# A two-block transformer kernel: another order of work in the opening of its first weight product

## What is computed

```python
def first_block(x, c, ada_w, ada_b, pre_g, post_g, sgu_w_in, ...):
    cond = jax.nn.silu(c)
    for i in range(DEPTH):
        mod = cond @ ada_w[i] + ada_b[i]
        shift, scale, gate = jnp.split(mod, 3, axis=-1)
        h = rms_norm(x, pre_g[i]) * (1 + scale[:, None, :]) + shift[:, None, :]
        ...
        y = sgu_mixer(h, sgu_w_in[j], ...)

def sgu_mixer(h, w_in, norm_g, w_s, b_s, w_out):
    u, v, z = jnp.split(h @ w_in, 3, axis=-1)
    ...
```

## Time and profile before

| | |
|---|---|
| median of 3 runs | 2480.13 us (2478.33 to 2480.51) |
| the profiled execution | 2477.93 us |
| its span | 2476.1 us |
| TensorE busy | 2433.2 us, 98% |
| VectorE busy | 1889.0 us, 76% |
| ScalarE busy | 1399.4 us, 57% |
| GpSimd busy | 442.0 us, 18% |
| granted TensorE clock, mean | 0.999 |

### The profile page before, as it was taken

How to read it: one execution, slowest core, us unless ns; L and a number is a source line. 1 busy time by engine, 2 the same in 40 slices (tenths; PEclk the granted TensorE clock), 3 DMA queues, 4 the chain that set the end, 5 groups by cost and what they waited for, 6 DMA issues and landing times.

```text
span 2476.1 us, 31108 instructions
## 1 busy us (share of the span) xinstructions
PE 2433.2 (98%) x11597; PEld 2018.7 (82%) x11597; DVE 1889.0 (76%) x2295; ACT 1399.4 (57%) x1934; POOL 442.0 (18%) x298
## 2 busy tenths in 40 slices
PE   6999999999999999998999999999999999999999
PEld 5888888888887989887888888888888888888887
DVE  7899798977777787866655555557988878788884
ACT  6655765444447555555566676755655545555553
POOL 0264563111020000110000000043111021111111
PEclk9999999999999999999999999999999999999999
DMA  9999677978784877754555556455465555646454
GB/s 364 321 341 349 237 256 273 336 283 290 271 313 149 246 212 220 233 208 149 167 173 163 177 153 183 157 187 187 155 236 170 204 187 191 217 170 221 170 203 154
DMA packets 370999, 549.47 MB, mean 222 GB/s; under 512 B 31405, under 2 KB 158129, under 8 KB 370225
## 3 DMA queue, kind: packets, MB, share of 16 engines
q1 hardware_dynamic: 368688, 539.54, 64.6%
q10 hardware_dynamic: 1824, 6.04, 0.7%
q0 software_dynamic: 352, 2.11, 0.2%
HBM read 545.53 MB, written 2.11 MB: 221 GB/s over the span
## 4 chain that ended last, share of the span: by engine, by line
PE 88%; DVE 8%; ACT 2%; issue 1%; DMA 1%; SPq 0%; POOL 0%; DVEq 0%; ACTq 0%; POOLq 0%
PE ps L2393 48%; PE ps L2398 24%; DVE lo L1305 3%; PE ps L2423 2%; PE ps L2419 2%; PE ps L2420 2%; DVE ps L1330 1%; PE ps L2379 1%; PE ps L2378 1%; PE ps L2380 1%; DVE lo L1282 1%; DMA raw<-in_sgu_w_in 1%; PE ps L3007 1%; PE ps L2655 1%; ACT hi L630 1%
## 5 line engine op out<-in xcount | busy, mean ns | idle before, releaser
L1305 DVE TENSOR_TENSOR lo<-raw,hi 128x1024 fp32r<-128x1024 f32 x550 | 706.9, 1304 | 350.8 <-ACT hi L630 350.2
L630 ACT ACTIVATE hi<-raw 128x1024 fp32r<-128x1024 f32 x550 | 571.3, 1051 | 431.3 <-PE ps L2398 352.7
L2393 PE MATMUL ps<-hi,a_hi 128*128 128x512 f32 (+1 forms) x2016 | 798.6, 396 | 2.1 <-issue 0.9
L2393 PE MATMUL ps<-hi,a_lo 128*128 128x512 f32 (+1 forms) x2016 | 785.6, 390 | 0.0
L2398 PE MATMUL ps<-lo,a_hi 128*128 128x512 f32 (+1 forms) x2016 | 539.0, 389 | 1.5 <-DVE lo L1305 1.5
L616 ACT ACTIVATE hi<-raw 128x1024 fp32r<-128x1024 f32 x339 | 358.2, 1060 | 292.7 <-PE ps L2398 255.2
L1282 DVE TENSOR_TENSOR lo<-raw,hi 128x1024 fp32r<-128x1024 f32 x339 | 424.4, 1272 | 107.2 <-ACT hi L616 105.0
L2393 PEld LDWEIGHTS ps<-hi,a_hi 128*128 128x128 f32 x2016 | 378.7, 188 | 85.1 <-issue 5.3
L2398 PEld LDWEIGHTS ps<-lo,a_hi 128*128 128x128 f32 x2016 | 378.4, 188 | 81.1 <-DVE lo L1305 1.9
L2393 PEld LDWEIGHTS ps<-hi,a_lo 128*128 128x128 f32 x2016 | 378.9, 188 | 74.4
L2393 PE MATMUL ps<-hi,b_hi 128*128 128x512 f32 x880 | 347.4, 395 | 0.6 <-ACT y L1015 0.3
(11 more groups left out here) (351 smaller groups left out, 2436.6 us busy)
## 6 DMA issues: line engine op xcount, KB each, us to landing
raw<-in_sgu_w_in SPq DMA_DIRECT2D x88, 1024.0 KB
raw<-in_ada_w SPq DMA_DIRECT2D x64, 1024.0 KB
raw<-in_w_up SPq DMA_DIRECT2D x64, 1024.0 KB
raw<-in_w_down SPq DMA_DIRECT2D x64, 1024.0 KB
raw<-in_w_in SPq DMA_DIRECT2D x42, 1024.0 KB
raw<-in_ada_w SPq DMA_DIRECT2D x64, 512.0 KB
raw<-in_sgu_w_out SPq DMA_DIRECT2D x32, 1024.0 KB
raw<-in_w_in SPq DMA_DIRECT2D x128, 256.0 KB
```

The costliest lines, as they stand in the source:

```text
L630: nc.scalar.activation(hi[:, q % CHUNKS, 0:width], raw[:, r % RAWS, q % 2 * CW:q % 2 * CW + width], ACT.Copy).then_inc(hi_ready, 1)
L1305: nc.vector.tensor_tensor(lo[:, q % CHUNKS, 0:width], raw[:, r % RAWS, q % 2 * CW:q % 2 * CW + width], hi[:, q % CHUNKS, 0:width].bitcast( ...
L2393: nc.tensor.matmul(ps[:, 2 * s + t, 0:width], x[:, k0 + j, t * P:(t + 1) * P], hi[:, c, w], start=begins, stop=False)
```

## The change

- **Head.** c goes to `acc_s` instead of `tf`, so SyncE no longer waits for GpSimd before it. The second half of x is issued by SyncE, behind slabs (0, 0) and (0, 1), with a semaphore of its own; the eight small vectors follow behind it. VectorE copies the small vectors only after all four sums of group 0.
- **x in pieces.** ScalarE normalises the first 512 columns of both halves, and the other 1536 later, between the first chunks. TensorE turns two groups of x before the first chunk (before: five) and the other six after chunks 1, 2, 3, 8, 9 and 10 (`XT_AFTER`; before: three, after chunks 1, 2 and 3).
- **Blocks.** LATE is 6: the first six chunks are one turn each, all of group 0. `GROUP_AFTER`, `SUMMED_AFTER` and the loads of the last slabs ("s") have new places. On ScalarE, `modulated(1)` stands in the turn of the loop for chunk 4 as before, but chunk 4 now ends a turn.
- **VectorE.** `modulated(0)` stands ahead of the first two lo; `split(0)` stands behind lo of chunk 0, then slab (1, 0), then lo of chunk 1.
- **Spatial turns** stand after chunks 43, 49, 55 and 61 instead of 45, 49, 53 and 57.

```diff
-GROUPS, LATE = 8, 4
-GROUP_AFTER = {4: 1, 14: 2, 24: 3, 36: 4, 46: 5, 58: 6, 66: 7}
+GROUPS, LATE = 8, 6
+GROUP_AFTER = {5: 1, 14: 2, 24: 3, 34: 4, 44: 5, 54: 6, 62: 7}
...
-    order = [(j, 0) for j in range(LATE)] + [(4, 0), (5, 0), (4, 1), (5, 1)] + [(j, h) for j in range(6, PHASE_W) for h in range(2)]
+    order = [(j, 0) for j in range(LATE)] + [(LATE + e, h) for h in range(2) for e in range(2)]
+    order += [(j, h) for j in range(LATE + 2, PHASE_W) for h in range(2)]
...
-XT_BANKS = (3, 4, 2, 3, 4, 4, 4, 4)
+XT_BANKS = (3, 4, 4, 4, 4, 4, 4, 4)
+XT_AFTER = (1, 2, 3, 8, 9, 10)
...
-            sp.wait_ge(set_up, 2)
-            sp.dma_start(ra[A_C:A_C + 16], d["c"].rearrange("a (r q) -> (a r) q", q=P)).then_inc(first_landed, 16)
+            sp.dma_start(c_rows, d["c"].rearrange("a (r q) -> (a r) q", q=P)).then_inc(first_landed, 16)
...
-                if r == 1:
+                if r == 2:
+                    sp.dma_start(x[:, 1, :], d["x"][0, P:2 * P, :]).then_inc(x1_landed, 16)
+                    sp.wait_ge(set_up, 2)
                     for place, source in small:
...
             x_turned(0)
+            x_turned(1)
             hi_next(act, n, 0)
+            modulated(0)
             hi_next(act, n, 1)
-            x_turned(1)
-            modulated(0)
+            normal(0, NB, D)
             hi_next(act, n, 2)
-            for g in range(2, 5):
-                x_turned(g)
-            group_at = {c + (c > 4): g for c, g in GROUP_AFTER.items()}
+            normal(1, NB, D).then_inc(n_out, 1)
+            group_at = {c + (1 if g > 1 else -1): g for c, g in GROUP_AFTER.items()}
             for q, (m, j, h, begins, ends) in enumerate(OPENING):
                 p = m // PHASE_W
                 act_steps(act, n, 1)
+                if q - 1 in XT_AFTER:
+                    x_turned(2 + XT_AFTER.index(q - 1))
...
             ada_sum(dve, n, 0, acc, early)
+            ada_sum(dve, n, 1, acc, early)
+            first_var()
+            ada_sum(dve, n, 2, acc, early, between=first_rstd)
+            ada_sum(dve, n, 3, acc, early)
             dve.wait_ge(vec_turned, 2)
             nc.vector.tensor_copy(va[:, KT:A_ROWS], ps[:, 4, KT:A_ROWS]).then_inc(vec_kept, 1)
             nc.vector.tensor_copy(vb[:, :], ps[:, 4, P:P + B_ROWS]).then_inc(vec_kept, 1)
-            ada_sum(dve, n, 1, acc, early, between=first_var)
-            ada_sum(dve, n, 2, acc, early, between=first_rstd)
-            ada_sum(dve, n, 3, acc, early)
...
+            modulated(0)
+            opening_lo(0)
+            split(0)
+            n.raw.base += 1
+            ada_sum(dve, n, 0, acc_s, early)
+            n.raw.base -= 1
+            opening_lo(1)
...
-            pe.wait_ge(n_out, 2)
-            x_turned(2)
             pe_ada(pe, n)
-            x_turned(3)
-            x_turned(4)
-            unread(0, 3)
+            unread(0, 5)
...
-                if 1 <= q < 4:
-                    x_turned(4 + q)
+                if q in XT_AFTER:
+                    pe.wait_ge(n_out, 2)
+                    x_turned(2 + XT_AFTER.index(q))
```

More of the change, by code:

```diff
@@ L194 @@
 OPENING = opening_chunks()
-SPATIAL_AFTER = tuple(next(q for q, c in enumerate(OPENING) if c.turn == 2 * PHASE_W + j and c.ends) for j in range(0, 8, 2))
-XT_BANKS = (3, 4, 2, 3, 4, 4, 4, 4)
+SPATIAL_AFTER = tuple(next(q for q, c in enumerate(OPENING) if c.turn == 2 * PHASE_W + j and c.ends) for j in range(0, PHASE_W, 3))
+XT_BANKS = (3, 4, 4, 4, 4, 4, 4, 4)
+XT_AFTER = (1, 2, 3, 8, 9, 10)
 def opening_slabs():
@@ L206, in opening_slabs @@
             slabs.append(sums.pop(0))
-        if FIRST - PHASE_W <= w < FIRST - PHASE_W + LAST_A:
-            slabs.append(("s", w - FIRST + PHASE_W))
+        if w in LAST_SUMMED_AFTER:
+            slabs.append(("s", LAST_SUMMED_AFTER.index(w)))
     assert not sums
@@ L863, in modulated @@
             def modulated(g):
+                act.wait_ge(xt_kept, g + 1)
                 act.wait_ge(scales, g + 1)
@@ L1674, in end_of_block @@
                                                    in1=rstd[:, :], op0=ALU.mult, op1=ALU.mult).then_inc(centred, 1)
-            ready = {c + 3 - (c == 4): g for c, g in GROUP_AFTER.items()}
+            ready = {c + (3 if g > 1 else 1): g for c, g in GROUP_AFTER.items()}
             last_ends = {q: c.block for q, c in enumerate(OPENING) if c.ends and c.turn >= 3 * PHASE_W}
@@ L1690, in opening_lo @@
                     end_of_block(last_ends[q - AHEAD])
-            for slab in OPENING_SLABS[4:]:
-                if slab[0] == "w":
-                    w = slab[1]
-                    opening_lo(2 * w)
-                    opening_lo(2 * w + 1)
-                    if w == 0:
-                        modulated(0)
-                else:
-                    out_ = acc if slab[0] == "s" else (acc, acc_s)[slab[1] % 2]
-                    ada_sum(dve, n, slab[-1], out_, early, between=(lambda: split(0)) if slab == ("a", 1, 0) else None)
+            modulated(0)
[5 more added lines that the diff above has]
+            opening_lo(1)
+            for slab in OPENING_SLABS[6:]:
+                if slab[0] == "w":
+                    opening_lo(2 * slab[1])
+                    opening_lo(2 * slab[1] + 1)
+                else:
+                    ada_sum(dve, n, slab[-1], acc if slab[0] == "s" else (acc, acc_s)[slab[1] % 2], early)
             for q in range(2 * FIRST, 2 * FIRST + AHEAD):
@@ L2596, in x_turned @@
             def x_turned(g):
-                if g >= 3:
-                    pe.wait_ge(xt_kept, g - 2 if g < 5 else g)
+                if g >= 2:
+                    pe.wait_ge(xt_kept, g)
                 for k in range(2 * g, 2 * g + 2):
```

29 lines of the change are left out of this document (15 added, 14 removed).

## The result

| | before | after |
|---|---|---|
| median | 2480.32 us (2478.33 to 2482.56, 6 runs) | 2498.47 us (2496.57 to 2500.05, 6 runs) |
| profiled execution | 2477.93 us | 2500.05 us |
| its span | 2476.1 us | 2498.2 us |

The ratio is 1.0072, with an interval of 1.0059 to 1.0085: slower by 18.2 us. The forecast was 2490.9, with a range up to 2497.

A forecast was written before the change was run, and what follows sets the result against it. TensorE, busy for 98% of the span, was taken to bound the kernel. The terms 0.2 + 5.6 + 0.3 + 3.2 + 1.3 + 0.2 gave 10.8 us more, 2490.9 us on the median, range 2484 to 2497.

The forecast's parts named there:

- Step 1: Head: the first chunk comes no sooner, at about 29.7, since TensorE's turning waits for VectorE's small-vector copies; +0.2 us.
- Step 2: Before chunk 3: the fifth slab's place is freed late, the load queue runs dry; +5.6 us, +0.3 one slab later.
- Step 3: Before chunk 6: TensorE waits for a turn's taking out, behind the second modulation on ScalarE; +3.2 us.
- 4, three more turnings: Between the first chunks: six groups of x are turned there instead of three, 3 x 0.44; +1.3 us.
- Step 5: Rest of the opening: 2.6 us of new wait, against old waits of 1.5 and 0.9 going; net +0.2 us.
- The extra 0.3 one slab later: Part of the supply hole: slab 3 lands at 46.4, its rounding and copy end just after TensorE ends chunk 3; +0.3 us.
- rival B: TensorE's clock slows after each of the two new waits: 4.8 us more, 2495.7; chance 13%.
- its term for VectorE's extra work: Ahead of chunk 44: one slab of ada_w more (24 instead of 23) on VectorE without slack; 2.6 us of wait.
- Rival C: VectorE falls behind in the dense stretch, by the upper bound for the rest of the opening: 2494.7; chance 12%.
- A: From 97 us on VectorE's own work sets the pace and swallows the early delay: no change, 2480.3; chance 12%.
- D: Head: sums run at VectorE's pace, not the loads', ending 2.8 us sooner: 2488.1; chance 8%.

The follow-up runs named there:

- d1: The kernel before, with nothing changed but a comment, profiled once more: 2481.53 us, span 2479.7.
- d2: The changed kernel, profiled once more: 2498.74 us, span 2496.9.
- a3: The changed kernel with VectorE's copies of the small vectors directly behind the variance, ahead of slab (0, 2): 2496.04 us, ratio 1.0058.
- a1: The changed kernel with lo of chunk 1 ahead of slab (1, 0) on VectorE: 2493.65 us, ratio 1.0049.
- a4: The changed kernel with unread products on TensorE, 22 behind chunk 2 and 14 behind the sum of group 1: 2493.84 us, ratio 1.0053.
- a2: The changed kernel with turn 4 taken out of its banks ahead of modulated(1) on ScalarE: 2497.66 us, ratio 1.0069.
- b3: The changed kernel with modulated(1) behind the taking out of turns 4 and 5 on ScalarE: 2496.82 us, ratio 1.0066.
- c2: The kernel before with the change's tables (six early blocks, group sums, last slabs, spatial turns), head of before kept: 2488.3 us, ratio 1.0034.
- b2: The changed kernel with the sums of groups 4 to 7 and the slabs back to a spread near the old one: 2500.35 us, ratio 1.0081.
- c1: The changed kernel with the tables of before (four early blocks, group sums, last slabs, spatial turns), head of the change kept: 2491.94 us, ratio 1.0049.

## Why the prediction was right or wrong

d1 and d2 are two executions near their medians (0.7 and 0.3 us above), so the terms are measured between them, by the marks:

| step | forecast | d2 less d1 |
|---|---|---|
| 1, first chunk | +0.2 | +0.2 (chunk 0) |
| 2, hole in the supply | +5.9 | +7.6 (chunk 0 to 3): wait 5.7, slow products 2.0 |
| 3, six blocks | +3.2 | +5.7 (3 to 7): wait 3.3, the rest slow products |
| 4, three more turnings | +1.3 | +1.5 (7 to 11) |
| 5, rest of the opening | +0.2 | +1.8 (11 to 96) |
| sum | +10.8 | +16.9 |

**Step 1 was right in cause**: the sums end at 23.2 in spite of their start at 8.86, and the copies behind them hold TensorE (a3). Sums that end at 22.7, as forecast, were 0.5 off, and so was the first chunk, at 30.2 and not 29.7: 0.55 later in d2 than in d1. That the mark shows +0.2 is luck, since the products of d2's first chunk came to full pace after six and those of d1's after eight.

**Step 2's chain was right link by link**: lo of chunk 1 at 32.6, issue at 33.87, slab 2, two roundings and a turn taken out, the copy. Slab 2 was there at 42.4 and not at 41.0: the issue came 0.5 us later, and the landing 8.5 us behind it and not 7.6. The wait was no longer for that, since TensorE, slow in chunk 0, came to it later too: the match of 5.7 with 5.6 is partly luck. (The prediction's count for eight slabs stands once as 29.8 and once as 29.3; nothing in the sum hangs on it.) The Trainium skill (DMA: Bandwidth & Descriptors, "Anatomy of one DMA") fits transfers that GpSimd issues, and these are SyncE's; by it the landing would have taken 6.8 us, and the measurement, 8.5, decides. a1 shows the cause by taking most of it away. The extra 0.3 one slab later did not come as a wait (chunk 3 was slow itself); where chunk 3 was fast, in a4, it was 0.9.

**Step 3 was right** to 0.1 us, in both kernels that have the tables. a2 and b3 show what the prediction did not work out: the modulation can't be moved to where it costs nothing. It only hands its wait to a later turn or to the supply.

**The step that failed is the price of the two long waits in steps 2 and 3.** The sum took each at its length and put nothing for slow products behind it; this was left to rival B, with 13% and 4.8 us. It came nearly whole: 2.0 and 2.5 us between d1 and d2, of which a4 took 3.4 back. The argument that failed was the one against it, that waits of 1 us in the trace are followed by full pace. It spoke of waits at most a third as long, while the only long idle times in the trace, in the head, were all followed by half pace. The nearer rows were those.

**Step 5 was short in its term for VectorE's extra work** (2.6 us). The prediction counted slabs of ada_w at chunk 44, one more than before. Up to the slab of chunks 48 and 49 there are two more (18 in `SUMMED_AFTER` against 16), and the old table had two pairs of chunks without one there (23 and 24). VectorE has no idle time left in that stretch. Its groups of lo, before from 155 to 250 us and after from 172 to 267 (two fences, columns as in the earlier trace rows):

```profile
L1305 DVE TENSOR_TENSOR lo<-raw,hi 128x1024 fp32r<-128x1024 f32 x34 | 51.1, 1532 | 7.1 <-ACT hi L630 7.1
```

```profile
L1317 DVE TENSOR_TENSOR lo<-raw,hi 128x1024 fp32r<-128x1024 f32 x31 | 53.4, 1754 | 0.6 <-ACT hi L635 0.6
```

Idle time of 7.1 us became 0.6, and a lo took 0.2 us longer on the mean. The two old waits (1.5 on lo, 0.9 on the turned weights) went, as forecast; 3.2 to 5.5 us of new ones came. By the table of marks, chunk 11 to 64 took 3.2 us more than in d1 in d2, 4.1 in c2 and 5.6 in the first profile of after, and chunk 64 to 96 took 1.4 less in all three. d2's listed waits are no longer than d1's (3.2 against 3.4), so part of its loss is in chunks that came some tenths late. That the spread of the slabs makes the loss before chunk 64 is shown by b2, where it went; that the two further slabs are what it consists of is argued from the count. Rival C came in part: over the forecast of step 5 the late loss was 1.6 us in d2, 2.5 in c2 and 4.0 in the first profile, where C had 3.8.

**Rivals A and D were wrong.** The delay was not swallowed: in c1, which has little else, 11.5 us at chunk 11 are still 11.1 at chunk 96 (against d1). Only a2's small gain was. The head was not quicker: slab (0, 0) came early (8.86), but slab (0, 2) not before 17.0.

**The base.** The forecast set its sum on one execution and added 2.2 us for the median. That execution was the luckier kind (d1), which the prediction could not see from one profile. Its median basis, 2480.13, was right to 0.2, so this cost the forecast nothing. But whoever takes the cost from the two first traces reads 22.1 us, where the medians differ by 18.2.

The mechanisms of steps 1 to 4 stand; what the sum lacked was the clock, and enough for VectorE. The forecast was 7.6 us low: some 4.5 for the clock, 1.6 for the late waits, and 1.5 by which the medians lie further apart than the executions d1 and d2 (the sum of their steps is 16.9, the medians differ by 18.2, and 0.2 is the base). Rival B added to the forecast makes 2495.7, inside the range. B and C together, which the prediction never had in one case, make 2499.5.

## What to carry to other kernels

A wait of several microseconds on TensorE was mostly paid twice here, once as the wait and once in slow products behind it: price it at its length and some 1 to 2.5 us more, and let independent products run in it where it can't be removed. Where one engine feeds the DMA queue by freeing places, find the last instruction that frees the next place and ask what was put ahead of it; one lo of 1.2 us, moved behind a slab, cost some 3 us of wait and the slow products behind it (a1). And where several mechanisms are each likely, some belong in the sum and not all among the rivals, since they come together.
